# Compression stage: a gate tile moved ahead of the first compression product, modulation columns summed in four column groups, scores over both key sets at once

## The reference, cut to what matters

```python
mod = jax.nn.silu(c) @ w_ada[l] + b_ada[l]
sh1, sc1, g1, sh2, sc2, g2 = jnp.split(mod[:, None, :], 6, axis=-1)
...
def compress(k, pos_emb, w1, w2):
    blocks = k[:, :, idx] + pos_emb
    flat = blocks.reshape(*blocks.shape[:3], CMP_BLOCK * HEAD_DIM)
    return jax.nn.gelu(flat @ w1) @ w2
...
kc = compress(k_cmp, cmp_pos_k, cmp_w1_k, cmp_w2_k)
vc = compress(v_cmp, cmp_pos_v, cmp_w1_v, cmp_w2_v)
o_cmp, p_cmp = nsa_compressed(q_a, kc, vc, slopes)
...
y = jax.nn.sigmoid(merge[:, :, 0]) * y_a + jax.nn.sigmoid(merge[:, :, 1]) * y_b
```

## Time and profile before

| | us |
|---|---|
| median of 3 runs | 1865.29 |
| lowest and highest run | 1858.76, 1869.38 |
| span of the profiled execution | 1863.9 |
| TensorE busy in it | 1720.4 (92%) |
| VectorE, ScalarE busy | 802.8 (43%), 528.4 (28%) |
| stretch of `stage_compress` in it | 183.9 to about 273.3 |

### The profile page before, as it was taken

How to read it: one execution, slowest core, us unless ns; L and a number is a source line. 1 busy time by engine, 2 the same in 40 slices (tenths; PEclk the granted TensorE clock), 3 DMA queues, 4 the chain that set the end, 5 groups by cost and what they waited for, 6 DMA issues and landing times. The chain is left out here.

```text
span 1863.9 us, 20172 instructions
## 1 busy us (share of the span) xinstructions
PE 1720.4 (92%) x8167; PEld 1181.4 (63%) x8167; DVE 802.8 (43%) x1272; ACT 528.4 (28%) x890; POOL 50.1 (3%) x89
## 2 busy tenths in 40 slices
PE   2999899889988999999979999999799989898888
PEld 2888776646677888888868886757334434343346
DVE  4763338742373222255642275234423323232345
ACT  4212237641152222232443252323100000000037
POOL 0000001000000000000000000000200000000000
PEclk9999789989998999999989999999999999999999
DMA  9675220012331332221322111227799999999961
GB/s 350 222 262 185 74 89 1 1 68 91 120 106 46 107 114 96 91 102 68 118 86 90 46 46 46 91 94 317 277 421 423 426 425 425 427 426 426 427 274 45
DMA packets 87799, 351.74 MB, mean 189 GB/s; under 512 B 9927, under 2 KB 39283, under 8 KB 71578
## 3 DMA queue, kind: packets, MB, share of 16 engines
q1 hardware_dynamic: 85146, 346.08, 47.8%
q0 software_dynamic: 2560, 4.37, 0.7%
HBM read 346.03 MB, written 8.43 MB: 190 GB/s over the span
## 5 line engine op out<-in xcount | busy, mean ns | idle before, releaser
L561 DVE TENSOR_TENSOR arena<-ring,arena 128x1024 fp32r<-128x1024 f32 x120 | 146.9, 1225 | 237.6 <-ACT arena L610 219.5
L2726 PE MATMUL ex_h<-ring,u_big_tail 128*64 128x512 f32 x512 | 153.7, 609 | 12.8 <-DMA ring<-in_w 7.9
L566 PE MATMUL up_ps<-h_high,arena 128*128 128x512 f32 x352 | 137.9, 392 | 6.9 <-PEq L192 6.3
L567 PE MATMUL up_ps<-arena 128*128 128x512 f32 x352 | 137.6, 391 | 0.0
L568 PE MATMUL up_ps<-h_high,arena 128*128 128x512 f32 x352 | 137.4, 390 | 0.0
L610 ACT CAST arena<-ring 128x1024 fp32r<-128x1024 f32 x82 | 85.8, 1047 | 161.9 <-PE up_ps L568 85.6
L2726 PE MATMUL ex_h<-s_ab,u_big_tail 128*64 128x512 f32 x272 | 114.3, 596 | 2.2 <-DVE u_big_tail L2697 1.4
L2697 DVE TENSOR_TENSOR u_big_tail<-ex_x,vcol 128x512 f32<-128x512 f32 x32 | 20.6, 686 | 180.0 <-PE ex_x L2690 180.0
L2726 PEld LDWEIGHTS ex_h<-ring,u_big_tail 128*64 128x64 f32 x512 | 47.0, 140 | 78.6 <-issue 77.7
L2992 ACT ACTIVATE u_big_tail<-ex_h 128x512 f32<-128x512 f32 x16 | 9.6, 598 | 293.8 <-PE ex_h L2726 293.8
L566 PEld LDWEIGHTS up_ps<-h_high,arena 128*128 128x128 f32 x352 | 66.5, 189 | 21.6 <-issue 6.6
(11 more groups left out here) (576 smaller groups left out, 3586.6 us busy)
## 6 DMA issues: line engine op xcount, KB each, us to landing
ring<-in_w SPq DMA_DIRECT2D x42, 2048.0 KB, 32.4
s_ab<-in_w SPq DMA_DIRECT2D x32, 2048.0 KB, 32.0
ring<-in_w_in SPq DMA_DIRECT2D x19, 2048.0 KB, 9.0
ring<-in_w_ada SPq DMA_DIRECT2D x24, 1024.0 KB, 6.8
reg_a<-in_w SPq DMA_DIRECT2D x10, 2048.0 KB, 31.4
w1flat<-in_w SPq DMA_DIRECT2D x10, 2048.0 KB
ring<-in_w_ffn_gate SPq DMA_DIRECT2D x11, 1024.0 KB, 5.4
ring<-in_w_ffn_up SPq DMA_DIRECT2D x11, 1024.0 KB, 8.0
```

Of the source, the lines that this page charges most:

```text
L561: return engine.tensor_tensor(lo, v, hi.bitcast(F32), ALU.subtract)
L566: nc.tensor.matmul(ps, x[0], y[0], start=start, stop=False)
L567: nc.tensor.matmul(ps, x[0], y[1], start=False, stop=False)
L2726: mm = nc.tensor.matmul(ps[half, :], xT[:, k, half], ws[j][:, k, cols], start=(k == 0), stop=(k == k_end - 1))
```

## The change

All of it is in `stage_compress`.

1. On TensorE the small transposes come right behind `gate(0)`, then `gate(1)`, then the sums; the two compression products stand next to each other, with nothing between.
2. The column sums are made by 4 matmuls of 512 columns. The weights are 32 columns of ones, and matmul j writes to partitions 32j to 32j+31 of one bank, so it uses a quarter of the array's columns. ScalarE copies the bank to `flat`, and four 128x128 transposes behind the row sums put the sums on partitions. VectorE picks column 0 of each group of 32.
3. The scores take the even and odd heads' keys in one matmul: 16 matmuls of 64 columns in place of 32 of 32 columns. A bank now holds two query blocks, and VectorE's addition reads it without a stride.
4. VectorE and ScalarE follow: weights for `gate(1)` and `gate(2)` are made first, VectorE makes all 16 additions in a row, then the weights' low part for `gate(2)`, and then moves the column sums.

```diff
             gate(0)
             pe.wait_ge(b.p1_even, 12)
             pe.wait_ge(b.p1_odd, 11)
-            for i in range(2 * KD):
-                mm = nc.tensor.matmul(ps_s[0][:, i:i + 1], b.acc2[:, D + i * P:D + i * P + P], b.ones[:, 0:1], start=True, stop=True)
-            mm.then_inc(mod_cols, 1)
+            pe.wait_ge(b.cmp_in, 16 * 12)
+            for i in range(2):
+                mm = nc.tensor.transpose(ps_pos[:, 32 * i:32 * i + 32], posr[:, 2 * i * HD:2 * (i + 1) * HD], b.ident[0:32, 0:32])
+            mm.then_inc(kcp, 1)
+            gate(1)
+            for j in range(4):
+                mm = nc.tensor.matmul(ps_s[0][32 * j:32 * j + 32, :], b.ones[:, 0:32], b.acc2[:, D + j * CH:D + (j + 1) * CH],
+                                      start=True, stop=True)
+            mm.then_inc(mod_sums, 1)
             for i, bank_ in enumerate(row_banks):
                 c = i // 2 * 3 * D + i % 2 * CH
                 mm = nc.tensor.matmul(bank_[:], b.ones[:], b.acc2[:, c:c + CH], start=True, stop=True).then_inc(mod_rows, 1)
             pe.wait_ge(mod_rows, 4)
             nc.tensor.sem_inc(b.ring_used[3], 1)
-            pe.wait_ge(b.cmp_in, 16 * 12)
-            for i in range(2):
-                mm = nc.tensor.transpose(ps_pos[:, 32 * i:32 * i + 32], posr[:, 2 * i * HD:2 * (i + 1) * HD], b.ident[0:32, 0:32])
-            mm.then_inc(kcp, 1)
+            pe.wait_ge(mod_flat, 1)
+            for c in range(4):
+                mm = nc.tensor.transpose(ps_s[0][:, c * P:(c + 1) * P], flat[:, c * P:(c + 1) * P], b.ident[:])
+            mm.then_inc(mod_cols, 1)
             pe.wait_ge(moved_rows, 2)
             for i in range(2):
-                if i:
-                    gate(1)
                 pe.wait_ge(win, i + 1)
...
             for t in range(NT):
-                for h in range(HEADS):
-                    at = (t * HEADS + h) // 2 * NC
-                    mm = nc.tensor.matmul(ps_s[h % 2][:, at:at + NC], b.qT[:, h // 2, t * P:t * P + P],
-                                          kc[:, h % 2, h // REP, :], start=True, stop=True)
+                for n in range(4):
+                    at = (t % 2 * 4 + n) * 2 * NC
+                    mm = nc.tensor.matmul(ps_s[t // 2][:, at:at + 2 * NC].rearrange("p (o n) -> p o n", o=2),
+                                          b.qT[:, n, t * P:t * P + P], kc[:, :, n // 2, :], start=True, stop=True)
...
+            parts.dve_w(dve, g0 + 1)
             dve.wait_ge(b.h_saved, 16)
-            dve.wait_ge(mod_cols, 1)
-            link(nc.vector.tensor_copy(b.modcol[:, 2 * KD:4 * KD], ps_s[0][:, 0:2 * KD]))
...
-                parts.dve_w(dve, g0 + 1 + i)
+            parts.dve_w(dve, g0 + 2)
+            dve.wait_ge(mod_cols, 1)
+            link(nc.vector.tensor_copy(b.modcol[:, 2 * KD:4 * KD].rearrange("p (j c) -> p j c", j=4),
+                                       ps_s[0][:].rearrange("p (c j r) -> p j c r", c=4, j=4)[:, :, :, 0]))
...
+            parts.act_w(act, g0 + 1)
             act.wait_ge(b.p1_even, 12)
             nc.scalar.activation(b.gate[:], b.gate[:], ACT.Sigmoid).then_inc(gsig, 1)
+            parts.act_w(act, g0 + 2)
+            act.wait_ge(b.h_saved, 16)
+            act.wait_ge(mod_sums, 1)
+            nc.scalar.copy(flat, ps_s[0][:]).then_inc(mod_flat, 1)
             for i, bank_ in enumerate(row_banks):
                 act.wait_ge(mod_rows, i + 1)
                 nc.scalar.copy((b.g1row, b.g2row)[i // 2][:, i % 2 * CH:i % 2 * CH + CH], bank_[:]).then_inc(moved_rows, 1)
-            parts.act_w(act, g0 + 1)
             keep(0)
-            parts.act_w(act, g0 + 2)
+            parts.act_w(act, g0 + 3)
             keep(1)
-            parts.act_w(act, g0 + 3)
```

More of the change, by code:

```diff
@@ L897, in stage_compress @@
     nc, a = b.nc, b.a
-    mod_cols, mod_rows, moved_cols, moved_rows = (b.sem(f"cmp_{n}") for n in ("mcols", "mrows", "mcolout", "mrowout"))
+    mod_sums, mod_flat, mod_cols, mod_rows, moved_cols, moved_rows = (
+        b.sem(f"cmp_{n}") for n in ("msums", "mflat", "mcols", "mrows", "mcolout", "mrowout"))
     b.cmp_moved_d, b.cmp_moved_a = b.sem("cmp_oad"), b.sem("cmp_oaa")
@@ L913, in stage_compress @@
     csum, cfac = (b.hTflat[:, i:i + NT * HEADS].rearrange("p (t h) -> p t h", t=NT) for i in (2432, 2464))
+    flat = b.hTflat[:, 3072:3072 + CH]
     pTc = b.hTflat[:, 0:2 * NT * P].rearrange("p (t g q) -> p t g q", t=NT, g=2)
@@ L1021, in link @@
                 dve.wait_ge(vz, n[0])
+            parts.dve_w(dve, g0 + 1)
             dve.wait_ge(b.h_saved, 16)
-            dve.wait_ge(mod_cols, 1)
-            link(nc.vector.tensor_copy(b.modcol[:, 2 * KD:4 * KD], ps_s[0][:, 0:2 * KD]))
-            nc.vector.sem_inc(moved_cols, 1)
-            nc.vector.scalar_tensor_tensor(out=b.mulcol[:, KD:2 * KD], in0=b.modcol[:, 3 * KD:4 * KD], scalar=1.0,
-                                           in1=b.vcol[:, VAT["norm_ffn_g"]:VAT["norm_ffn_g"] + KD], op0=ALU.add, op1=ALU.mult)
             nc.vector.memset(kp[:, :, :, :, NCMP:NC], 0.0)
@@ L1045, in _ @@
                 last.then_inc(win, 1)
-                parts.dve_w(dve, g0 + 1 + i)
+            parts.dve_w(dve, g0 + 2)
+            dve.wait_ge(mod_cols, 1)
+            link(nc.vector.tensor_copy(b.modcol[:, 2 * KD:4 * KD].rearrange("p (j c) -> p j c", j=4),
+                                       ps_s[0][:].rearrange("p (c j r) -> p j c r", c=4, j=4)[:, :, :, 0]))
+            nc.vector.sem_inc(moved_cols, 1)
+            nc.vector.scalar_tensor_tensor(out=b.mulcol[:, KD:2 * KD], in0=b.modcol[:, 3 * KD:4 * KD], scalar=1.0,
+                                           in1=b.vcol[:, VAT["norm_ffn_g"]:VAT["norm_ffn_g"] + KD], op0=ALU.add, op1=ALU.mult)
             dve.wait_ge(sel, 2)
@@ L1062, in _ @@
             dve.wait_ge(sc, 1)
-            for odd in range(2):
-                c = cs[:, :, odd::2, :]
-                last = nc.vector.tensor_tensor(c, c, ps_s[odd][:].rearrange("p (t h n) -> p t h n", t=NT, h=HEADS // 2), ALU.add)
+            for i in range(2):
+                c = cs[:, 2 * i:2 * i + 2]
+                last = nc.vector.tensor_tensor(c, c, ps_s[i][:].rearrange("p (t h n) -> p t h n", t=2, h=HEADS), ALU.add)
             link(last)
```

2 lines of the change are left out of this document (1 added, 1 removed).

## The result

| | before | changed |
|---|---|---|
| median of the runs, us | 1865.29 | 1855.87 |
| lowest and highest run | 1858.76, 1869.38 | 1854.48, 1857.91 |
| span of the profiled execution | 1863.9 | 1853.9 |
| mean granted clock of TensorE in it | 0.972 | 0.975 |

Both medians are of five runs. The ratio is 0.994 (95% interval 0.9924 to 0.9955), 9.4 us less. The forecast was 22.1 us less, 1843.2, and its range ended at 1852.

What follows compares the result with a forecast made beforehand. The prediction took TensorE's own time to bound `stage_compress`; its new steps summed to 46.61 us against 68.73, and the 22.1 us less, taken from the median 1865.3, gave 1843.2 us, range 1837 to 1852.

Steps and rivals of the forecast that it cites:

- The sum for the stage: TensorE's steps in `stage_compress`, small transposes to softmax transposes, would sum to 46.61 us against 68.73, 22.1 us less.
- five steps of 0.43 us: Column sums in `stage_compress`: second record of one matmul overlaps only the first of the next, taking 2.15 us.
- the lower bound: Column sums in `stage_compress`: if four column groups ran all at once, two records' time, 0.86 us.
- The rival in which the groups run one by one: Column sums in `stage_compress`: column groups would not overlap, +1.3 us, 1844.5; no separate chance given.
- a drain at a change of tiling mode: Column sums on TensorE: changing the tiling mode drains the engine; the forecast added nothing for it.
- The cover on VectorE: VectorE's additions would be ready at 198.0, ahead of the first product at 201.4; cover 3.4 us, at least 2.1.
- The clock rival: TensorE's clock falls in the two compression products, giving 1848 us or, if it falls sooner, 1853.7; chance 0.18.
- The absorbed gain: Behind the stage, say in a transfer not starting earlier, the gain is lost wholly (1865) or half (1854); chance 0.04.
- Of transfers I was right: Experts' weight loads, issued when earlier buffers come free, would start earlier by the same amount, 22 us.
- I pass it on whole: From the stage to the kernel's end: the full 22.1 us gain reaches the end, giving 1843.2 us.

Runs made afterwards that it cites:

- N = 26: Changed kernel with 26 idle one-column fp32 matmuls (104 instructions) on TensorE in a wait ahead of the first stage; 1843.45 us, ratio 0.9884.
- 13 or 26 matmuls: Changed kernel with idle TensorE matmuls: 13 ahead of the first stage (1840.77 us, again 1846.46), 13 in the router stage (1845.81), or 26 ahead of the first stage (1843.45).
- changed, third: Changed kernel measured a third time without an edit, on the same chip as the two kernels with 13 idle matmuls; 1851.77 us, ratio 0.9917.
- the two with 13: Changed kernel with 13 idle matmuls on TensorE, ahead of the first stage (1846.46 us) or in the router stage (1845.81 us), on one chip.
- 13 matmuls in the router: Changed kernel with 13 idle one-column matmuls on TensorE in the router stage, where it waits for VectorE; 1845.81 us, ratio 0.9888.
- the late loads: Changed kernel with three weight loads of the last stage issued from SyncE only after the last block's work; 1852.35 us, ratio 0.9928.
- N = 38: Kernel before with 38 idle one-column matmuls (152 instructions) on TensorE in a wait ahead of the first stage; 1879.17 us, ratio 1.0066.
- N = 6: Changed kernel with 6 idle one-column matmuls (24 instructions) on TensorE ahead of the first stage; 1845.94 us, again 1850.99 us.

## Why the forecast was wrong, point by point

**The sum for the stage held.** From the small transposes to those of the softmax it was forecast at 46.61 us and took 45.46 (189.55 to 235.01):

| us | forecast | measured |
|---|---|---|
| small transposes | 0.28 | 0.24 |
| `gate(1)` | 5.53 | 5.66 |
| column sums | 2.15 | 1.00 |
| row sums and wait | 3.74 | 3.85 |
| four transposes | 0.40 | 0.46 |
| products and wait | 7.66 | 7.56 |
| `gate(2)`, layer, `gate(3)` | 11.91 | 11.96 |
| scores | 3.68 | 3.48 |
| `gate(4)`, `gate(5)`, wait | 11.26 | 11.25 |

**The one term that was off is the column sums**, and by a wrong reading of the earlier trace rows. I let the two records of one matmul run in turn with the next one's, five steps of 0.43 us. In the trace of after, the first records of all four matmuls start within 20 ns of each other and the second ones 0.45 us later, also together: eight records of about 604 ns in 1.00 us. That is the lower bound that I had stated, 0.86, plus 0.14. The Trainium skill (TensorE: Matmul & The Clock Gate, Part 3) says that matmuls in different tiles of the array run at the same time and that a pack lasts hardly longer than one matmul; the trace agrees, with 1.00 us. The rows of after, by line (ns: smallest, median, largest):

```profile
L965 PEld LDWEIGHTS cmp_s<-ring,ones x8: 106/108/109, 195.5 to 195.5; 128*32 128x32 f32 x8
L965 PE MATMUL cmp_s<-ring,ones x8: 592/604/617, 195.5 to 195.9; 128*32 128x512 f32 x8
```

The rival in which the groups run one by one fell with it, and a drain at a change of tiling mode, of which the Trainium skill (TensorEngine Tiling, Key Properties) speaks, is not seen as a cost: the row sums, which use the whole array again, begin 1.00 us after the sums, so it could only be part of the 0.14 us above the bound.

**The cover on VectorE held.** Its sixteen additions end ahead of the first product, and its moves of the column sums stand behind the low part, unneeded for long:

```profile
190.22 8.27 DVE L1044 TENSOR_TENSOR reg_b<-reg_a,s_ab 64x248 f32<-64x248 f32 x16
198.53 1.23 DVE L561 TENSOR_TENSOR p_w<-ring,p_w 128x1024 fp32r<-128x1024 f32 x1
200.96 0.17 DVE L1050 COPY modcol<-cmp_s 128x16 f32<-128x16 f32 x1 [1.21 <-PE cmp_s L975]
```

8.27 us, against 8.1; they end at 198.49, 2.3 us ahead of the product at 200.76. With the sums at their lower bound I had said 2.1.

**The clock rival fell.** It had a chance of 0.18. Two products in a row, 7.3 us of 64-column matmuls, ran at 1.00, and so did all from 120.9 to 359.8 us.

**The absorbed gain fell too, in the form that I gave it.** GpSimd's first work of attention waited 201.7 us for `gate(7)` where it waited 224.7, the 23 us of the stage:

```profile
POOL u_big L1396 <- PE cmp_f L568: 201.7, 1, 201.7
```

And in the kernel with N = 26, 23.1 us at the stage's end are still 22.9 at 1780, through 500 us of experts' weights that come by DMA. Of transfers I was right: they start earlier by about what the work ahead gains (the first load of the last stage at 1751.3 us where it was 1768.6).

**The step that failed is "I pass it on whole".** It asked who waits for a result, a buffer or a transfer, and found nothing to absorb the gain; but an engine also waits for its own code. Taking the three traces of the changed kernel against the four with 13 or 26 matmuls, the first lose 7.6 to 8.8 us at the branch and the second gain 1.5. Of these 9 to 10 us the branch itself is 5.6 to 6.1 (6.15 to 6.65 against 0.51). The rest is the clock: between 1750 and 1810 the changed kernel runs 10.2, 13.7 and 13.7 us at half clock, the four others none.

**How much of the median is that?** Every run lists its span and mean clock. Between runs of one kernel, a thousandth of the mean clock less goes with 1.2 us more; it is 3.7 us of half clock, so one microsecond at half clock goes with about a third of one in time. This is a correlation, which no run tests by itself. The 17 runs of the changed kernel have a mean span of 1851.8 at a clock of 0.9753, the 16 runs with 13 matmuls, in either place, 1842.4 at 0.9791. Of the 9.4 us between them, 0.0038 of clock is 4.6 us, and 4.8 remain at equal clock, somewhat less than the 5.6 to 6.1 us that the branch costs in the three traces. But these runs come from several chips. Where kernels ran beside each other:

| beside each other | apart, us | by the clock | at equal clock |
|---|---|---|---|
| changed, N = 26 | 10.2 | 5.5 | 4.7 |
| changed, third, and the two with 13 | 6.4 | 2.4 | 4.0 |

So the fetch takes 4 to 5 us of the lost gain each time, and half clock 2 to 6 more, which differs from chip to chip or hour to hour. In the traces the greater part of the half clock that the padded kernels lack between 1750 and 1810 us stands right behind the fetch.

**What stays open.** Another 6.8 us of half clock, between 1270 and 1750, shows in all three traces of the changed kernel and in none with 13 or 26 matmuls (10.2 against 3.4); I didn't find what starts it. About 1 us is lost between 1110 and 1140 (0.9 to 1.5 us) in the three traces of the changed kernel and in the one with 13 matmuls in the router, which lie behind that place, and hardly any in those with 13 or 26 at the start (0.0 to 0.1). All four have there a wait for issue of 0.7 to 1.3 us, the late loads one of 0.3, the other kernels with the change none; the changed kernel's:

```profile
PE mx_f L543 <- issue: 0.7, 1, 0.7
```

The kernel before with N = 38, whose code stands in the same place modulo 256, has it as well (1.1 us). That fits the place of the code once more, but no q8 packet arrives just then, so what it is stays open. And the half clock in attention differs from trace to trace (23.9, 17.1 and 13.7 us for the changed kernel, 0 with the late loads, 0 to 3.4 with N = 6), and between 380 and 420 us the traces without it gain 5.4 and 5.5 us where others lose up to 2.9; no edit explains it.

## What to carry to other kernels

Where a program is long and has a runtime branch on a critical engine, code that is added or removed anywhere ahead of it can move the time by several microseconds. Before a small edit is judged, read the duration of every branch in both traces, and if it jumped from half a microsecond to several, pad the list with a few idle instructions in a wait and measure again: here 13 idle matmuls turned 0.6 to 0.8% into 1.1 to 1.4%. Count half clock over the whole span, too: the change took 30.6 us of it out of the stage, but by the mean clocks of the two traces (0.9718 and 0.9754) their half clock is some 105 us before and still some 91 after (estimates). So read the mean clock of each run beside its time, and repeat a kernel on another chip: one kernel's median moved by up to 5.7 us.

## What the runs showed of the hardware that I had not expected

A conditional branch on TensorE costs 0.42 to 0.51 us, or 3.45 to 6.65 us when a packet of code has to come first: 2.4 to 2.7 us from the start of its packet of 16,384 bytes, and 0.75 to 4.1 us until this packet starts. The same edit in the kernel before, 152 instructions added, made it 0.66% slower.

Four fp32 matmuls of 512 columns in four groups of 32 array columns take 1.00 us together, hardly more than one alone (0.86): both records of each overlap with those of the others. And 16 one-column matmuls in their place cost 3.9 us more in the stage: they take 3.70 us against 1.00 and the 0.46 of the transposes, and 3.4 us of half clock come with them.
